# A two-stack transformer: the compressed/selected/window layer as one phase of turns, and bias, scale and maximum of the scores in one VectorE pass

## The reference

```python
def nsa_attention(h, w_in, w_out, cmp_pos, cmp_w1, cmp_w2, rel_table):
    # 16 heads of 64 in 4 groups; six key/value projections and three gates a head
    q, kc, vc, ks, vs, kw, vw, gate = jnp.split(h @ w_in, splits, axis=-1)
    kc_b = compress_kv(kc, cmp_pos[0], cmp_w1[0], cmp_w2[0])   # 15 blocks of 32 keys, gelu MLP
    vc_b = compress_kv(vc, cmp_pos[1], cmp_w1[1], cmp_w2[1])
    p_cmp = masked_softmax(q @ kc_b * scale, cmp_end <= t)
    o_cmp = p_cmp @ vc_b
    o_slc = selected_block_attention(q, ks, vs, sel_idx, rel_table)  # all 4 blocks are chosen
    o_win = banded_attention(q, kw, vw, rel_table, 512)              # wider than the sequence
    g = jax.nn.sigmoid(gate)                                         # three for each head
    return (g0 * o_cmp + g1 * o_slc + g2 * o_win) @ w_out
```

## Time and profile before

| | before |
|---|---|
| median of 3 runs | 3479.1 us (3475.09 to 3480.41) |
| profiled execution | 3480.2 us |
| its span, first to last instruction | 3478.1 us, 53492 instructions |
| TensorE busy | 3352.5 us (96%) |
| VectorE busy | 2099.3 us (60%) |
| ScalarE busy | 1716.9 us (49%) |
| mean granted TensorE clock | 0.983 |
| read from memory | 615.62 MB, 180 GB/s over the span |

### The profile page before, as it was taken

One profiled execution on the slowest core, in us unless ns is written; L12 is line 12 of the kernel. 1 busy time (PEld: TensorE's weight loads), 2 busy tenths in 40 slices (PEclk: granted clock), 3 DMA queues, 4 the chain that ended last, 5 costly groups with the idle time before them and its releaser, 6 DMA issues. The chain is left out here.

```text
span 3478.1 us, 53492 instructions
## 1 busy us (share of the span) xinstructions
PE 3352.5 (96%) x20376; PEld 2963.9 (85%) x20376; DVE 2099.3 (60%) x2315; ACT 1716.9 (49%) x2279; POOL 81.0 (2%) x180
## 2 busy tenths in 40 slices
PE   8999999999999999999999999899999999999899
PEld 6899988888998888887888888788888888888787
DVE  5567565656766555566565564665656755656655
ACT  4456444444664444455444433454445544445544
POOL 0000000000000000000000000000000000000000
PEclk9999999999999999999999987999999999999999
DMA  6665445555554555553555542245555445555354
GB/s 243 219 222 206 147 174 187 187 191 184 196 179 149 190 192 183 181 185 143 182 193 182 181 158 79 81 182 191 183 191 194 147 170 192 182 192 189 128 192 170
DMA packets 105214, 618.78 MB, mean 178 GB/s; under 512 B 10832, under 2 KB 19152, under 8 KB 34800
## 3 DMA queue, kind: packets, MB, share of 16 engines
q1 hardware_dynamic: 84288, 562.07, 44.8%
q10 hardware_dynamic: 20784, 54.71, 4.7%
HBM read 615.62 MB, written 9.50 MB: 180 GB/s over the span
## 5 line engine op out<-in xcount | busy, mean ns | idle before, releaser
L1291 DVE TENSOR_TENSOR wlo<-raw,whi 128x2048 fp32r<-128x2048 f32 x526 | 1204.7, 2291 | 657.8 <-ACT whi L760 655.5
L1982 PE MATMUL ps<-xhl,whi 128*128 128x512 f32 x3456 | 1201.9, 396 | 0.0
L760 ACT CAST whi<-raw 128x2048 fp32r<-128x2048 f32 x526 | 1001.1, 1904 | 204.7 <-PE ps L2118 108.7
L1986 PE MATMUL ps<-xhl,wlo 128*128 128x256 f32 x3456 | 893.1, 279 | 0.0
L1982 PEld LDWEIGHTS ps<-xhl,whi 128*128 128x128 f32 x3456 | 626.5, 188 | 121.7
L1986 PEld LDWEIGHTS ps<-xhl,wlo 128*128 128x128 f32 x3456 | 651.6, 189 | 37.5
L2117 PE MATMUL ps<-wlo,ht 128*128 128x512 f32 x1056 | 417.1, 395 | 0.0
L2116 PE MATMUL ps<-whi,ht 128*128 128x512 f32 x1056 | 417.1, 395 | 0.0
L2118 PE MATMUL ps<-whi,ht 128*128 128x512 f32 x1056 | 416.6, 394 | 0.0
L2097 PE MATMUL ps<-xhl,whi 128*128 128x256 f32 x1360 | 393.7, 289 | 9.4 <-DVE qb L1701 5.4
L2099 PE MATMUL ps<-xhl,wlo 128*128 128x256 f32 x1360 | 388.3, 286 | 0.0
(11 more groups left out here) (299 smaller groups left out, 3868.0 us busy)
## 6 DMA issues: line engine op xcount, KB each, us to landing
raw<-stream SPq DMA_DIRECT2D x528, 1024.0 KB, 4.8
bias<-rel_bias ACTq DMA_DIRECT2D x80, 256.0 KB, 2.6
gain<-gains ACTq DMA_DIRECT2D x19, 1024.0 KB, 4.8
bias<-fixed_bias ACTq DMA_DIRECT2D x40, 256.0 KB, 3.2
rel_bias<-rel_vectors SPq DMA_DIRECT2D x16, 512.0 KB
x<-x_tokens ACTq DMA_DIRECT2D x1, 1024.0 KB, 5.0
y_tokens<-x ACTq DMA_DIRECT2D x1, 1024.0 KB, 3.9
s<-constants ACTq DMA_DIRECT2D x1, 512.0 KB, 6.5
```

The source lines that it names most:

```text
L760: nc.scalar.copy(whi[:, slot, :], raw[:, slot, :]).then_inc(sem["hi_ready"], 1)
L1291: nc.vector.tensor_tensor(wlo[:, slot, :], raw[:, slot, :], whi[:, slot, :].bitcast(F32), ALU.subtract).then_inc(sem["lo_ready"], 1)
L1982: wide = lambda: pe.matmul(ps[:, bank, 0:2 * half], hi[:, k, col0:col0 + P], src[:, k0 + k, :], start=first and k == 0, stop=last and k == ...
L1986: e = pe.matmul(ps[:, bank, 0:half], lo[:, k, col0:col0 + P], src[:, k0 + k, 0:half], start=False, stop=False)
```

## The change

1. The compressed/selected/window layer becomes one phase, `nsa`, of 32 turns. `NSA` lists what lies between the turns: products, the four hidden steps, block keys and values, block scores, turning and values of the compressed part, output steps, with the banks each uses and the engine that empties it. `NSA_SLOTS` deals their parts over the turns. A group of four heads has its selected turns, then its window turns. `keep_busy` and POOL's staging of queries are gone from this layer; behind it, `arrive` idles 18 transposes and not 5.
2. The source of the compression is copied by ScalarE, and so are `kcb` and `vblk`; POOL clears `vblk` and `pcmp`. Gates come from Tanh and a VectorE step, and not from Sigmoid. The compressed result is added to `o` in turn 22 (`NSA_ADD`), Gelu runs in turn 13.
3. In `mix`, `weave` and `nsa`, the add and the maximum are one VectorE instruction for each half of the tokens, only as wide as the half has keys: `tensor_tensor_reduce`, s = -scale x (scores + bias) with the minimum kept as `nmax`, starting from the negated sink or 3e38. The exponential has scale -1. Bias tables are stored 8 times as large and sinks negated. The semaphore `biased` is gone; `scores` and `turn_heads` wait for `max_ready`.

```diff
+NSA_EARLY = 4
+NSA_SLOTS = slots_of([(n, part) for n in range(NSA_EARLY, len(NSA) - 1) for part in range(NSA[n].parts)][:-1],
+                     [4, 4, 4, 2, 2, 2, 2, 2, 2, 2, 2, 2, 2, 2, 3, 0, 1, 0, 0, 1, 1, 1, 0, 0, 0, 2, 2, 2, 2, 0, 1, 1, 1, 0, 0])
+NSA_TURNS = {23: 0, 24: 1, 25: 2, 26: 3, 27: 4, 29: 5, 32: 6, 34: 7}
+NSA_GELU = 13
+NSA_ADD = 22
+def nsa_items():
+    one = lambda kind, at, bank, by: Item(kind, at, 1, (bank,), 4, by)
+    items = [one("v", 0, 4, "act"), one("q", 0, 5, "dve"), one("k", 0, 6, "dve"), Item("gate", 0, 1, (7,), 2, "act"),
+             one("cmp", 0, 4, "act"), one("cmp", 1, 5, "act"), one("k", 4, 6, "dve"), one("v", 256, 7, "act"),
+             one("q", 4, 4, "dve"), Item("hidden", 0, 2, (5, 6), 4, "dve"), one("q", 8, 7, "dve"),
+             Item("hidden", 1, 2, (4, 5), 4, "dve"), one("q", 12, 6, "dve"), Item("blocks", 0, 0, (4,), 1, "act"),
+             Item("cmp_scores", 0, 0, (7,), 1, "dve"), Item("cmp_turn", 0, 0, (5, 6), 1, "act"), Item("cmp_values", 0, 0, (7, 4), 1, "add"),
+             Item("cmp_values", 1, 0, (5, 6), 1, "add")]
+    items += [Item("out", i, 1, (), 4, "") for i in range(4)]
...
 plan():
-            project(t("v", 0, 256, 8, 1, 1), f("q", 0, 4), f("cmp", 0, 2))
-            add("compress", ("pe", "act", "dve"), 4,
...
-            project(f("k", 0, 1), f("k", 4, 1), t("v", 256, 256, 8, 1, 1), t("gate", 0, 48, 8, 1, 1))
-            add("cmp_attend", ("pe", "act", "dve"),
...
-            attend("nsa_slc", HEADS, "causal", 0)
-            attend("nsa_win", HEADS, "causal", 0)
...
-            turn(0, 8)
-            wout()
+            nsa()
...
 VectorE, biased(t) of weave (mix and nsa alike, mix with 256 keys in both halves):
-                    nc.vector.scalar_tensor_tensor(
-                        out=s[:, parity, :, 0:T], in0=ps[:, parity, :].rearrange("p (a b) -> p a b", a=TT),
-                        scalar=scale, in1=bias[:, parity, :, :], op0=ALU.mult,
-                        op1=ALU.add).then_inc(sem["biased"], 1)
-                    dve.wait_ge(sem["biased"], B["biased"] + t + 1)
-                    nc.vector.tensor_reduce(nmax[:, 2 * parity:2 * parity + 2], s[:, parity, :, 0:width], AX.X,
-                                            ALU.max, negate=True).then_inc(sem["max_ready"], 1)
+                    for qt in range(TT):
+                        n = 2 * parity + qt
+                        e = nc.vector.tensor_tensor_reduce(
+                            out=s[:, parity, qt, 0:keys_of(ph, qt)], in0=ps[:, parity, qt * T:qt * T + keys_of(ph, qt)],
+                            in1=bias[:, parity, qt, 0:keys_of(ph, qt)], scale=-scale, scalar=UNBOUNDED if sink is None else sink,
+                            op0=ALU.add, op1=ALU.min, accum_out=nmax[:, n:n + 1])
+                    e.then_inc(sem["max_ready"], 1)
...
 TensorE, nsa, the loop of turns:
+                for t in range(ph.n + 3):
+                    here = NSA_SLOTS[t]
+                    first = (len(here) + 1) // 2
+                    if t < ph.n:
+                        scores(t)
+                    if t in NSA_TURNS:
+                        turn_heads(NSA_TURNS[t], t)
+                    for n, part in here[:first]:
+                        part_of(n, part)
+                    if 1 <= t <= ph.n:
+                        turn_probs(t - 1)
+                    for n, part in here[first:]:
+                        part_of(n, part)
+                    if 2 <= t <= ph.n + 1:
+                        values(t - 2)
...
 VectorE, nsa, the same:
+                    if t < ph.n:
+                        biased(t)
+                    if t == NSA_ADD:
+                        compressed_added()
+                    if t in NSA_TURNS:
+                        turned(NSA_TURNS[t], (t + 1) % 2)
+                    follow(here[:first])
+                    if 1 <= t <= ph.n:
+                        inverted(t - 1)
+                    follow(here[first:])
+                    if 2 <= t <= ph.n + 1:
+                        heads_out(t - 2)
```

More of the change, by code:

```diff
@@ L748, in mix @@
                     of_head(k)
-            run(pool, "pool", dict(between=between, attend=attend, mix=mix))
+            run(pool, "pool", dict(between=between, nsa=nsa, mix=mix))
         @block.scalar
@@ new lines, in nsa @@
+                for n in range(NSA_EARLY):
+                    ahead(ph, NSA[n].step)
+                    empty(n)
+                for t in range(ph.n + 3):
+                    here = NSA_SLOTS[t]
+                    first = (len(here) + 1) // 2
+                    if t < ph.n:
[3 more added lines that the diff above has]
+                    if t in NSA_TURNS:
+                        turned(NSA_TURNS[t], (t + 1) % 2)
+                    follow(here[:first])
+                    if 1 <= t <= ph.n:
+                        inverted(t - 1)
+                    follow(here[first:])
+                    if 2 <= t <= ph.n + 1:
+                        heads_out(t - 2)
@@ L1964, in _ @@
+            run(dve, "dve", dict(setup=setup, between=between, ffn=ffn, mix=mix, nsa=nsa, weave=weave))
         @block.tensor
@@ L2023, in arrive @@
                 if tt == 0:
[L2024 removed]
+                    keep_busy(18 if before_of(last).kind in ("weave", "nsa") else 5 if last.after == "post" or last.final else 0, 3)
                 for half in range(2):
@@ L2708, in stream_of @@
+            run(pe, "pe", dict(setup=setup, ffn=ffn, mix=mix, nsa=nsa, weave=weave))
 def stream_of(a, n_steps):
```

1053 lines of the change are left out of this document (539 added, 514 removed).

## The result

The kernel before took 3478.4 us in this comparison, the changed one **3378.9 us** (3376.6 to 3388.7): ratio 0.972, 95% interval 0.9699 to 0.9741. A second comparison of the same two gave 3478.1 and 3381.9, ratio 0.973 (0.9714 to 0.9746).

A forecast was written before the change was run, and what follows sets the result against it. TensorE's work bounds almost everything, except the selected layer, with serial stages, idle seams and half clock. 3480.2 - 58 (selected layer) - 8 (fused pass) = 3414, the median 1.1 us lower: 3413 us, range 3383 to 3448.

The forecast's parts named there:

- The fused pass, its price: VectorE's single add-and-minimum pass in attention: 0.70 to 1.07 us a causal head, taken as 0.9, against 1.37 before.
- What follows from the cover: Window and moba layers: shorter VectorE pass shortens some six waits in each of three weaves, -8 us (0 to -18).
- Mixes at 0: Mix phases: TensorE idles only 4.4 of 261 us, so the fused pass gives 0, between +1 and -2.
- The selected layer, rebuilt: Selected layer in moba's form, costed from moba's measured 129.7 us plus terms and new waits: 208 us, 58 less than 266.4.
- Gate product: Selected layer's 48-column matmuls: 3.2 us at full and 4.2 at half clock, +7.3, plus 2 (0 to 5) behind it.
- the hidden steps: Selected layer's four compression steps (turns 7, 8, 11, 12): 64 pairs at full clock, +14 us; 28 at half clock.
- rival 1: Clock lower in the selected layer: hidden steps and sparse turns 17 to 24 at 1.2 GHz, +20 and +8, 3441 us; 17%.
- TensorE's hole in turn 3: Selected layer: wait behind VectorE's compression-block building; 3.9 us already in moba's base, the blocks add 3.5.
- the softmax: Selected layer, turn 16: compressed softmax on VectorE delays TensorE's values, +5.5 us, and 4 (0 to 10) for half clock behind.
- The nine sparse turns: Selected-layer turns with next to no product, paced by the chain of engines: 2.5 us each (2.3 to 2.9), +9 us.
- Rival 3: Fewer waits than set: half of the selected layer's 26 us goes, and the weaves give 18: 3390 us; 16%.
- Rival 2: The fused pass is dear: no gain in the weaves and +0.3 us in 20 chain-bound turns: 3427 us; 10%.

The follow-up runs named there:

- two_pass: Changed kernel with the fused VectorE pass undone in all phases (scale-and-add, then maximum, as before), new selected layer kept: 3416.4 us.
- extra_behind: Changed kernel plus an unused tile and one unneeded 0.735 us VectorE operation a head, behind the operation that signals `max_ready`: 3392.1 us.
- busy_holes2: two_pass plus idle TensorE transposes in moba's holes, 32 ahead of head 2's probabilities, 16 each ahead of the scores of heads 8 and 12: 3410.8 us.
- late_blocks: Changed kernel with VectorE building the compression blocks behind the score pass of turns 3 and 4, not at the end of turn 2: 3383.6 us.
- scrap_only: Changed kernel plus an unused 112-column tile, cleared once in setup, which shifts the buffers behind it; no extra operations: 3377.8 us.
- busy_holes: two_pass plus idle TensorE transposes in moba's holes, the first 32 misplaced by a turn, ahead of head 3's probabilities: 3416.7 us.

## Why the prediction missed, by its steps

The measured time is 34 us below the forecast. In the profiles 18 of them lie outside the selected layer (-26 where I had -8) and 15 in it (192.7 where I had 208).

- **The fused pass, its price.** Taken at 0.9 us for a causal head from ScalarE's accumulator read of 0.187; it is 0.56, the read 0.08 and hidden. Even the lower bound that I gave, 0.70, was too high: the durations of the two halves do sum to 0.71, but each starts 0.07 to 0.08 us before the one ahead of it ends, and I had summed durations where the path sees start to start. A mis-sized term.
- **What follows from the cover.** This step failed. I put -8 us on it, six waits in each of three layers and nothing for the mixes; it is -25. By `two_pass` some 13.6 us of it are waits and 11.1 are matmuls that ran slower before. So two things were missing. First, the waits: they are 13.6 us and not 8, because each head's pass got 0.77 us shorter and not 0.45, and because VectorE's queue behind the signal is waited for too, which I had not counted (`extra_behind`, 4.0 us of waits). Second, the clock, which I had put at nothing: the row of moba's 3.9 us hole and its clock of 0.94 were both in my hands, but I asked only of the selected layer what a hole does to the clock. Without its clock falls, and with the waits left, moba is 3.9 us shorter (`busy_holes2`). That they vanish altogether with the fused pass is in part luck: with the same hole of 2.77 us one came back in `late_blocks`.
- **Mixes at 0.** -3.8 in the first, -0.7 in the second: in the first, TensorE's idle time fell from 4.4 to 2.3 us and its busy time by 1.7 at a clock of 1.00 instead of 0.99. I had read 4.4 us idle of 261 as nothing to gain.
- **The selected layer, rebuilt.** By the prediction's measure I said 208 with the fused pass. With two passes it is 201 to 207, with the fused one 192.7 (195.3 in `scrap_only`). The sum of parts was therefore near, at its upper end, what the new form gives by itself, and what was missing is the fused pass in it: the base of 129.7 us was moba's with its own holes and clock falls, 8.5 us of which the pass took away, and I had noted that they were "in the 129.7" without asking whether they would stay. Most of the pass's part in this layer is clock: 12.3 of the 14.6 us between `two_pass` and the changed kernel.
- **Its single terms** held in the main. (As printed they add up to 182.1 and not 182.3 us, which changes nothing.) Gate product 5.4 us, nearly all at full clock (7.3 and 2 behind it said), block scores 10.9 us (11 said), the hidden steps at clock 1.00 (said; rival 1 falls), TensorE's hole in turn 3 5.4 us (3.9 + 3.5 said), the softmax 1.9 + 1.6 us (5.5 said) with some 6 us lost to the clock behind it (4 said), `compressed_added` 1.95 (2.5 said). The nine sparse turns were said at 2.5 us; they go from 1.5 to 4.8, turn 17 with the waits for the softmax to 6.9, so a flat pace was no good model.
- **The rivals.** Rival 3 (fewer waits, 3390) had the direction and two thirds of the way, with 16%. Rival 2 (the pass is dear) fell, and its opposite happened.

The gain of 99.5 us divides, by `two_pass`: 62 for the rebuilt layer alone (3478 to 3416) and 37.5 for the fused pass, 25 of it outside that layer. With the unused tile in both kernels the pass is worth 31.9 us (3409.7 to 3377.8), 22 outside.

## What to carry to other kernels

When a step is shortened that every head goes through, look for the holes that it shortens and read the granted clock in the windows behind each: a hole that gets shorter can give its own time and the half-speed stretch behind it, here one to one in moba. Part TensorE's time in waits and busy time before naming a cause, since the clock's part moved by several us between programs alike in moba or the selected layer, and the waits there by one at most. Don't take a neighbouring phase as a base for another without asking which of its stalls the same change removes. And a run of narrow matmuls can be made quicker by more work among it, which is worth trying before moving waits about; moving a wait in an in-order queue mostly moved it to the next turn.

## What I had not expected of the hardware

- A fused VectorE operation with accumulator takes 289 ns for 128 and 419 ns for 256 columns of PSUM and SBUF, 60 ns more with a start value from memory, and its accumulator read 82 ns, under the next operation.
- 128-column records among narrow ones held the clock at 1.00 where it fell to 0.50 on 15-column records alone, with TensorE busy all the time in both.
- The clock fell behind a hole of 2.77 us in one program and not in another with the same phase, and behind one of two holes of 2.02 us in one phase.
- Buffers placed 448 bytes further on make the 256-column products of the mixes 4 to 5 ns quicker, 2 to 4 us a phase. Why, these runs don't show.
- Two profiled executions of one program agree in 0.1 us in the selected and the moba phase; two programs that are alike in a phase can differ there by 1.5 us for one clock fall more (moba: 122.1 in the changed kernel, 123.6 in `late_blocks`) and by 6 for several (selected layer: 208.2 in `two_pass`, 201.8 in `busy_holes`).
